# One decoder layer on Trainium2: attention values stationary, probabilities streaming, already divided by their sums

## The reference

```python
xn = rms_norm(h, norm1_w);  proj = xn @ w_in          # q, k, v, gated-linear-attention parts, gate_a, gate_g
p  = softmax(concat([s_meta, s_band, sink]))          # 8 heads, 2 kv heads, window 128, 16 meta keys, 1 sink
o  = p_band @ v_band + p_meta @ v_meta                # per head, 64 wide
y_attn = o @ w_attn_branch;  y_gla = og @ w_gla_branch
merged = sigmoid(gate_a) * y_attn + sigmoid(gate_g) * y_gla
h = h + merged @ w_out
h = h + hierarchical_moe(rms_norm(h, norm2_w))        # 32 experts, 2 per token
```

## Time and profile before

| | us |
|---|---|
| median of the timed runs | 701.44 |
| the profiled execution, its own time | 705.6 |
| its span, first to last instruction | 703.7 |
| attention with the gate chunks and unit (18, u) | about 183 to 330 |
| branch products, merge | about 324 to 372 |
| output product, router | about 372 to 440 |
| experts | about 441 to 703.7 |

### The profile page before, as it was taken

One profiled execution on the slowest core, in us unless ns is written; L12 is line 12 of the kernel. 1 busy time (PEld: TensorE's weight loads), 2 busy tenths in 40 slices (PEclk: granted clock), 3 DMA queues, 4 the chain that ended last, 5 costly groups with the idle time before them and its releaser, 6 DMA issues.

```text
span 703.7 us, 11219 instructions
## 1 busy us (share of the span) xinstructions
PE 670.2 (95%) x4523; PEld 512.8 (73%) x4523; DVE 384.8 (55%) x717; ACT 202.1 (29%) x426; POOL 103.1 (15%) x131
## 2 busy tenths in 40 slices
PE   4999999999999999999999993999999999999998
PEld 2579999888788888888779992656566575756564
DVE  3537224687888777776764556352625253442515
ACT  4337123223533434332333333110111202020102
POOL 3400006788500000000000011110101010110000
PEclk9799999999999999999999996899999999999999
DMA  7432211301122111111347107799999999999953
GB/s 232 138 98 77 66 61 61 107 14 61 61 61 61 60 61 61 61 61 60 104 137 299 61 31 300 305 414 385 414 402 412 403 411 407 403 422 401 418 212 119
DMA packets 49797, 139.32 MB, mean 198 GB/s; under 512 B 6066, under 2 KB 28099, under 8 KB 41556
## 3 DMA queue, kind: packets, MB, share of 16 engines
q1 hardware_dynamic: 47298, 134.36, 50.3%
q0 software_dynamic: 2304, 4.20, 1.6%
q10 hardware_dynamic: 146, 0.07, 0.1%
HBM read 138.61 MB, written 4.19 MB: 203 GB/s over the span
## 4 chain that ended last, share of the span: by engine, by line
PE 86%; DVE 6%; ACT 3%; issue 2%; DMA 2%; POOL 0%; POOLq 0%; ACTq 0%; DVEq 0%
PE bank L881 16%; PE bank L562 13%; PE bank L563 12%; PE bank L564 12%; PE bank L894 8%; PE bank L989 7%; PE bank L789 2%; DVE y_lo L1688 1%; PE bank L762 1%; PE bank L788 1%; PE bank L787 1%; PE bank L722 1%; PE bank L726 1%; ACT whi L1098 1%; DVE sig_a L1436 1%
## 5 line engine op out<-in xcount | busy, mean ns | idle before, releaser
L1374 DVE TENSOR_TENSOR wlo<-wraw,whi 128x2048 fp32r<-128x2048 f32 (+1 forms) x26 | 58.7, 2258 | 30.9 <-ACT whi L1098 30.9
L562 PE MATMUL bank<-whi,xhi 128*128 128x256 f32 (+1 forms) x256 | 73.3, 286 | 0.0
L564 PE MATMUL bank<-whi,xlo 128*128 128x256 f32 (+1 forms) x256 | 71.7, 280 | 0.0
L563 PE MATMUL bank<-wlo,xhi 128*128 128x256 f32 (+1 forms) x256 | 71.7, 280 | 0.0
L562 PE MATMUL bank<-xhi,whi 128*128 128x512 f32 (+2 forms) x176 | 69.5, 399 | 1.6 <-DVE wlo L1374 1.6
L563 PE MATMUL bank<-xlo,whi 128*128 128x512 f32 (+2 forms) x176 | 68.2, 391 | 0.0
L564 PE MATMUL bank<-xhi,wlo 128*128 128x512 f32 (+2 forms) x176 | 67.6, 388 | 0.0
L881 PE MATMUL bank<-wgate,xgT 128*64 128x256 f32 x512 | 60.5, 390 | 1.3 <-DVE xgT L1656 1.0
L881 PE MATMUL bank<-wup,xgT 128*64 128x256 f32 x512 | 58.4, 381 | 0.0
L894 PE MATMUL bank<-wdown,hT 128*64 128x512 f32 x256 | 58.1, 595 | 0.0
L1098 ACT ACTIVATE whi<-wraw 128x2048 fp32r<-128x2048 f32 (+1 forms) x26 | 47.8, 1842 | 25.9 <-PE bank L564 18.7
(11 more groups left out here) (291 smaller groups left out, 1305.4 us busy)
## 6 DMA issues: line engine op xcount, KB each, us to landing
wgate<-in_expert_w_gate SPq DMA_DIRECT2D x32, 1024.0 KB, 7.4
wup<-in_expert_w_up SPq DMA_DIRECT2D x32, 1024.0 KB, 9.6
wdown<-in_expert_w_down SPq DMA_DIRECT2D x32, 1024.0 KB, 17.4
wraw<-in_w_in SPq DMA_DIRECT2D x17, 1024.0 KB, 5.6
wraw<-in_w_out SPq DMA_DIRECT2D x4, 1024.0 KB, 5.4
h<-in_x SPq DMA_DIRECT2D x4, 512.0 KB, 5.3
wraw<-in_w_gla_branch SPq DMA_DIRECT2D x2, 1024.0 KB, 5.2
wraw<-in_w_attn_branch SPq DMA_DIRECT2D x2, 1024.0 KB, 5.1
```

What stands on the lines that cost most here:

```text
L562: nc.tensor.matmul(ps, lhi(k), rhi(k), start=(k == 0), stop=False)
L563: nc.tensor.matmul(ps, lhi(k), rlo(k), start=False, stop=False)
L564: last = nc.tensor.matmul(ps, llo(k), rhi(k), start=False, stop=(k == kt - 1))
L1374: nc.vector.tensor_tensor(w_view(wlo[split_buffer(c)], c), w_view(wraw[c % 2], c), w_view(whi[split_buffer(c)], c).bitcast(F32), ALU.subtr ...
```

## The change

The list of steps changes: PV is made for two attention units at once, at the odd ones, and three units after the first of the two; the sigmoid of a gate unit is made one unit later; a new step ("share", b, i) stands behind it; onorm is gone, and oT has no transposes. In "share" VectorE adds sum and sink term of the two heads and takes the reciprocal, and ScalarE multiplies both heads' probabilities by it in place; the transposes wait for that. PV has the values stationary, 64 columns for each kv head, and the transposed probabilities of two units streaming, 256 wide; kv head 0 writes partitions 0 to 63 of the bank and head 1 the others, the two heads' products taking turns. The result has a row per feature, so ScalarE and VectorE take `ohi` and `olo` straight from that bank. The rows of w_attn_branch are reordered on the host for it. `pt` and `ptm` hold two units' probabilities and become twice as long.

```diff
         b, i = pairs[n]
-        return [("PV", b, i)] + ([("onorm", b)] if i == 3 else [])
+        return [("PV", b, i)] + ([("oT", b)] if i == 2 else [])
 
...
             b, i = pairs[n]
-            s += [("unit", c, u)] + (product(n - 2) if n >= 2 else [])
+            s += [("unit", c, u)] + (product(n - 3) if n >= 3 and n % 2 else [])
             s += [("S", b, i)] + ([("PT",) + pairs[n - 1]] if n >= 1 else [])
             if i == 2:
-                s += [("ogT", b)] + ([("oT", b - 1)] if b >= 1 else [])
-            s += [("sig", c, u)]
-    s += [("prep", 19), ("unit", 18, 0)] + product(14) + [("PT",) + pairs[15], ("unit", 18, 1)] + product(15)
-    s += [("unit", 18, 2), ("oT", NB - 1), ("unit", 18, 3)]
+                s += [("ogT", b)]
+            s += [("sig", 10 + (n - 1) // 2, (n - 1) % 2)] if n >= 1 else []
+            s += [("share", b, i)]
+    s += [("prep", 19), ("sig", 17, 1), ("unit", 18, 0), ("PT",) + pairs[15], ("unit", 18, 1)] + product(14)
+    s += [("unit", 18, 2), ("unit", 18, 3)]
     s += [("prep", 20)] + [("unit", 19, u) for u in range(4)]
...
         oglo = at("oglo", Y + 8 * K1, [P, 4, T], F32R)
-        ptm = [at(f"ptm{i}", 81 * K1 + 512 * i, [NM, P]) for i in range(2)]
         place = [Y + 16 * K1]
...
         v_tok = more("v_tok", [P, NB, P])
-        pt = [at(f"pt{i}", place[0] + K1 * i, [P, 256]) for i in range(2)]
+        pt = [at(f"pt{i}", place[0] + 2 * K1 * i, [P, 2, 2 * P]) for i in range(2)]
         k_tok = more("k_tok", [P, NB, P])
-        o_tok = at("o_tok", place[0], [P, 512])
         km = more("km", [NM, CW])
...
         att_stat = more("att_stat", [P, 2, 5, HQ])
+        ptm = [at("ptm0", 81 * K1, [NM, 2 * P]), more("ptm1", [NM, 2 * P])]
         norm1_b = at("norm1_b", G + 24 * K1, [P, D])
...
                             for b in range(NB):
-                                pe.wait_ge(*banks.emptied(("ogT" if name == "wg" else "oT", b)))
+                                pe.wait_ge(*banks.emptied(("ogT" if name == "wg" else "PV", b)))
                         ih, il = (oghi, oglo) if name == "wg" else (ohi, olo)
...
                         pv = banks.take(pe, "O", ("PV", b))
-                    for j in range(2):
-                        pe.wait_ge(*banks.emptied(("PT", b, i, j)))
-                        hd = j * 4 + i
-                        o = pv[:, hd * DH:(hd + 1) * DH]
-                        vc = slice(j * DH, (j + 1) * DH)
-                        if b > 0:
-                            nc.tensor.matmul(o, pt[j][:, 0:128], v_tok[:, b - 1, vc], start=True, stop=False)
-                        nc.tensor.matmul(o, pt[j][:, 128:256], v_tok[:, b, vc], start=(b == 0), stop=False)
-                        last = nc.tensor.matmul(o, ptm[j][:, :], vm[:, vc],
-                                                start=False, stop=True)
+                    for ii in (i, i + 1):
+                        for j in range(2):
+                            pe.wait_ge(*banks.emptied(("PT", b, ii, j)))
+                    heads = [(pv[j * DH:(j + 1) * DH, i * P:(i + 2) * P], slice(j * DH, (j + 1) * DH)) for j in range(2)]
+                    if b > 0:
+                        for j, (o, vc) in enumerate(heads):
+                            nc.tensor.matmul(o, v_tok[:, b - 1, vc], pt[j][:, 0, :], start=True, stop=False)
+                    for j, (o, vc) in enumerate(heads):
+                        nc.tensor.matmul(o, v_tok[:, b, vc], pt[j][:, 1, :], start=(b == 0), stop=False)
+                    for j, (o, vc) in enumerate(heads):
+                        last = nc.tensor.matmul(o, vm[:, vc], ptm[j][:, :], start=False, stop=True)
                     last.then_inc(s_pv, 1)
-                elif kind in ("oT", "ogT"):
+                elif kind == "ogT":
                     b = step[1]
-                    if kind == "oT":
-                        pe.wait_ge(*banks.emptied(("PV", b)))
-                    else:
-                        pe.wait_ge(s_ogn, b + 1)
-                    src = o_tok[:, :] if kind == "oT" else rgs[:, b, :]
+                    pe.wait_ge(s_ogn, b + 1)
                     ps = banks.take(pe, "unit", step)
                     for j in range(4):
-                        last = nc.tensor.transpose(ps[:, j * P:(j + 1) * P], src[:, j * P:(j + 1) * P], ident)
+                        last = nc.tensor.transpose(ps[:, j * P:(j + 1) * P], rgs[:, b, j * P:(j + 1) * P], ident)
                     last.then_inc(banks.done(step), 1)
...
                         nc.scalar.activation(p, p, ACT.Exp, bias=st_[:, 1, :], scale=SCALE,
-                                             accum_out=st_[:, 2, :]).then_inc(s_prob, 1)
+                                             accum_out=st_[:, 2, :]).then_inc(s_sum, 1)
                         nc.scalar.activation(st_[:, 3, :], sinks[:, hd:hd + 1], ACT.Exp,
                                              bias=st_[:, 1, :]).then_inc(s_es, 1)
+                elif kind == "share":
+                    _, b, i = step
+                    act.wait_ge(s_part, 4 * b + i + 1)
+                    for j in range(2):
+                        n = 2 * (4 * b + i) + j
+                        hd = j * 4 + i
+                        p = prob[n % 4][:, 128 if b == 0 else 0:272]
+                        nc.scalar.activation(p, p, ACT.Copy, scale=att_stat[:, b % 2, 4, hd:hd + 1]).then_inc(s_prob, 1)
                 elif kind == "PT":
...
                     act.wait_ge(*banks.filled(name))
-                    if 4 * b + i:
-                        act.wait_ge(s_pv, 4 * b + i)
+                    if 4 * b + i >= 2:
+                        act.wait_ge(s_pv, (4 * b + i) // 2)
                     ps = banks.get(name)
-                    c0 = 128 if b == 0 else 0
-                    nc.scalar.activation(pt[0][:, c0:256], ps[:, c0:256], ACT.Copy)
-                    nc.scalar.activation(ptm[0][:, :], ps[0:NM, 256:384], ACT.Copy).then_inc(banks.read(name), 1)
+                    k0, tok = 1 if b == 0 else 0, slice(i % 2 * P, (i % 2 + 1) * P)
+                    keys = ps[:, k0 * P:2 * P].rearrange("p (k t) -> p k t", t=P)
+                    nc.scalar.activation(pt[0][:, k0:2, tok], keys, ACT.Copy)
+                    nc.scalar.activation(ptm[0][:, tok], ps[0:NM, 256:384], ACT.Copy).then_inc(banks.read(name), 1)
                 elif kind in ("oT", "ogT"):
                     b = step[1]
-                    act.wait_ge(*banks.filled(step))
+                    name = ("PV", b) if kind == "oT" else step
+                    act.wait_ge(*((s_pv, 2 * (b + 1)) if kind == "oT" else banks.filled(step)))
                     dst, s = (ohi, s_ohi) if kind == "oT" else (oghi, s_oghi)
-                    ps = banks.get(step)[:, :].rearrange("p (j t) -> p j t", j=4)
+                    ps = banks.get(name)[:, :].rearrange("p (j t) -> p j t", j=4)
                     nc.scalar.activation(dst[:, :, b * P:(b + 1) * P], ps, ACT.Copy).then_inc(s, 1)
...
                     dve.wait_ge(*banks.filled(name))
-                    if 4 * b + i:
-                        dve.wait_ge(s_pv, 4 * b + i)
+                    if 4 * b + i >= 2:
+                        dve.wait_ge(s_pv, (4 * b + i) // 2)
                     ps = banks.get(name)
-                    c0 = 128 if b == 0 else 0
-                    nc.vector.tensor_copy(pt[1][:, c0:256], ps[:, c0:256])
-                    nc.vector.tensor_copy(ptm[1][:, :], ps[0:NM, 256:384]).then_inc(banks.read(name), 1)
-                elif kind == "onorm":
-                    b = step[1]
-                    st_ = att_stat[:, b % 2, :, :]
-                    dve.wait_ge(s_es, 8 * (b + 1))
-                    link(nc.vector.tensor_tensor(st_[:, 4, :], st_[:, 2, :], st_[:, 3, :], ALU.add))
-                    link(nc.vector.reciprocal(st_[:, 4, :], st_[:, 4, :]))
-                    dve.wait_ge(s_pv, 4 * (b + 1))
-                    if b:
-                        dve.wait_ge(*banks.filled(("oT", b - 1)))
-                    nc.vector.tensor_tensor(o_tok[:, :].rearrange("p (h d) -> p h d", d=DH),
-                                            banks.get(("PV", b))[:, :].rearrange("p (h d) -> p h d", d=DH),
-                                            st_[:, 4, :].unsqueeze(2).to_broadcast([P, HQ, DH]), ALU.mult)\
-                        .then_inc(banks.read(("PV", b)), 1)
+                    k0, tok = 1 if b == 0 else 0, slice(i % 2 * P, (i % 2 + 1) * P)
+                    keys = ps[:, k0 * P:2 * P].rearrange("p (k t) -> p k t", t=P)
+                    nc.vector.tensor_copy(pt[1][:, k0:2, tok], keys)
+                    nc.vector.tensor_copy(ptm[1][:, tok], ps[0:NM, 256:384]).then_inc(banks.read(name), 1)
+                elif kind == "share":
+                    _, b, i = step
+                    n = 4 * b + i
+                    sums, sink, both = (att_stat[:, b % 2, k, i:HQ:4] for k in (2, 3, 4))
+                    dve.wait_ge(s_es, 2 * (n + 1))
```

(10 more changed lines are left out.)

## The result

The changed kernel takes 722.6 us (median of 4 runs, 720.98 to 722.88), the kernel before, run beside it, 701.1 us (4 runs, 700.72 to 701.48): ratio 1.0276, 95% interval 1.0253 to 1.0298. It is 21.5 us slower. The prediction was slower by 13.8 us, 715.2 us; the measured time lies 2.1 us above its range. A later repeat gave 722.23 us, ratio 1.0286 (1.0265 to 1.0308).

The account below looks back on a forecast made before the run. TensorE was taken to bound the kernel before, VectorE and ScalarE in turn after the change. Delay of 11.7 us plus clock 2.1 made 13.8; added to the 701.44 us median, 715.2 us, range 709.5 to 720.5.

Parts of the forecast that it names:

- TensorE has 16 us less to do: Attention products and transposes: 27.9 us removed, 12 us of two-unit PV added; TensorE alone would win about 16 us.
- VectorE and ScalarE become the bound by order: Gate blocks: share behind the sigmoid delays ScalarE's Copies and conversions, VectorE waits; +5.5 us at the start of chunk 18.
- TensorE stays the bound: Rival for the gate blocks: conversions ready as today, TensorE's 16 us come out, 685.5 us; chance 0.05.
- The round of 37.4 us: VectorE's time per block of four units: 28.66 us of work plus 8.7 of waits, against 36.2 today.
- the upper of the bounds: ScalarE's scaled Copies in share: between 0.36 and 0.52 us each, middle 0.43 taken; bounds give +9.9 and +14.2 us.
- the prediction's own walk: Each engine followed in program order from the stage's start to the last split of the merged rows: +11.7 us.
- The tail: Chunk 18: last PV waits behind split and postponed sigmoid, +6.3 us, TensorE still for about 6.0.
- The clock: After the 6 us stop in chunk 18 the granted clock falls to 0.50: +2.1 us, bounds 0 and 5.
- a rival with a chance of 0.08: Clock also falls in the blocks' 3.3 us stops, three more times 2.1 us: 721.5 us; chance 0.08.
- There TensorE has 5 us a block to spare: Gate blocks: TensorE's slack of 5 us, given as the reason against the half clock costing time after shorter stops.
- The sum: Whole kernel: 11.7 us from the walk plus 2.1 for the clock, 13.8 us slower.

Follow-up runs that it names:

- The last kernel: Changed kernel with share ahead of each unit's own sigmoid, and chunk 18's last probability copies and unit (18, 2) moved earlier: 688.28 us, ratio 0.9805.
- early conversion: Changed kernel with ScalarE converting the next chunk's weights one step earlier, before its Copies; share left behind the sigmoid: 698.01 us.
- share first: Changed kernel with share ahead of the sigmoid and each sigmoid back in its own unit: 693.02 us.
- stops filled: Changed kernel with unread transposes where TensorE stood still, 28 in each block's third unit and 50 before the last PV: 719.37 us.
- tail reordered: Changed kernel with chunk 18's last sigmoid and probability copies ahead of chunk 19's split, and unit (18, 2) ahead of the last PV: 713.34 us.

## Why the prediction was right, and where its sizes were off

**TensorE has 16 us less to do.** Right. The last kernel takes 12.9 us less in the gates and 2.5 in the tail than before, 15.4 together. PV of two units takes 1.59 us (1.6 predicted). The twelve records alone are 1.31 at the 0.109 us of the earlier trace rows, which leaves 0.28 us for entering and leaving the shape. The Trainium skill (TensorEngine Tiling (Array Packing), section When to Use Tiling) recommends this swap, and its section Key Properties warns of the drain; the runs agree with the advice only where VectorE and ScalarE have their steps in the right order: 21.5 us slower in the one, 12.8 us faster in the other.

**VectorE and ScalarE become the bound by order.** Right, and shown twice: by moving share, and by moving the conversion. The rival "TensorE stays the bound" named its point of decision, 5.6 us of waits a block; the early conversion removed 2 x 2.80 and got 32.83 us, share first 32.17, with TensorE busy throughout (31.8 predicted for its round).

**The round of 37.4 us.** This is the step that was too small, and the main reason why the measured time lies above the range: 38.65 measured. Waits 2.80 + 2.81 for `whi` (2 x 2.69), 1.97 for `ohi` (1.86), 1.33 for `oghi` (1.4), and 0.93 for late transposes, where the prediction had 0.1: together 9.84 against 8.7; the work is the other 28.8 (28.66). So 0.83 of the 1.25 us is that last wait. Of it 0.51 is the half clock (0.42 remain with the stops filled). Of the other 0.74 us, 0.66 lie in waits behind the Copies: 0.32 at the transposes, 0.23 at the two splits, 0.11 at the output. They are put down to the Copies themselves, which took 0.51 us busy and 0.42 to the next start by their rows (two in 0.93 or 0.94, `whi` 0.84 us after the first starts, where 0.66 was walked). That is the upper of the bounds (0.52 and about 0.42), where the middle was taken, and by the prediction's own walk the upper bound is worth 2.5 us of the sum (14.2 in place of 11.7). That share was not tested by itself. The last 0.08 is work and rounding. By the third block the delay was 4.4 us where 3.0 was predicted, two blocks added 2.45 each where 1.25 was: 9.35 at (18, 0) against 5.5.

**The tail.** The order of events was right, step by step. TensorE was idle for 5.90 us before the last PV (6.0 predicted), and (18, 2) came at 18.10 us (16.2): the copies ended 0.5 us later than walked, and the last PV, at half clock, took 2.95 us in place of 1.6. From (18, 0) on the prediction has 11.7 - 5.5 = 6.2 us and the clock's 2.1, together 8.3; 9.0 was measured.

**The clock.** It did fall to 0.50 after the stop in chunk 18. The price of 2.1 us was about right: filling the stops shortened the tail by 1.9, with the two reservations made there. It fell as well after each of the blocks' stops of 3.0 to 3.1 us, which the prediction held to be a rival with a chance of 0.08 and a price of 2.1 us each. That rival's 721.5 us comes nearest to the measured time, but by luck: filling the four stops of the gates gave back 0.9 us and not 6.3. TensorE makes up most of what it loses there: with the tail reordered the half clock lasted longer (mean 0.94 in the gates against 0.96), and the gates took 146.16 us, against 146.20. It doesn't make up all of it, since the transposes stand right behind the stop and VectorE waits for them. "There TensorE has 5 us a block to spare" was the wrong reason: it has them on the average, not at that place.

**The sum.** 20.1 us between the two profiled executions (722.64 and 702.51) against 13.8 predicted: 3.9 more in the gates, 0.7 in the tail, 1.1 at one wait in the router, 0.6 in the experts. The last two the prediction put at nothing, and their cause is open. The other 1.4 us of the 21.5 is that the second profile of before lies that much above the median of the first comparison.

**Open.** The wait in the router is for the rows gathered by DMA, before and after the change, in TensorE's timeline:

```profile
435.66 1.97 PE L875 MATMUL bank<-cst,xg 128*128 128x128 f32 x8 [3.75 <-DMA xg<-rows_hbm,row_no]
```

```profile
455.21 1.97 PE L874 MATMUL bank<-cst,xg 128*128 128x128 f32 x8 [4.86 <-DMA xg<-rows_hbm,row_no]
```

The instructions there are the same, and so is their distance before the wait. Of the nine kernels with the new attention three have the short one (3.64 to 3.82 us), six and the repeat the long one (4.60 to 4.86). What decides it was not found. In the best kernel it takes back 0.9 us.

## What to carry to other kernels

Before work is handed over from an engine that is full to engines that have time, look where in their program the new instructions stand and what is queued behind them: here two Copies of 0.4 us waited for VectorE and held back a conversion of 1.9 us that VectorE needed for its next step, and moving one step of the list made +21 us into -3. A step that another engine waits for goes ahead of a long piece that nobody waits for. A mean slack of an engine is no cover for its slowest moment, and of the bounds of an unknown cost take the upper one when it lies in a loop that closes on itself.

## What the runs showed of the hardware that was not expected

- ScalarE's Copy with a scale per partition costs as much as an Exp of that shape: two of 128x272 in 0.93 us (0.51 busy and 0.42 to the next start), against 0.52 busy for the Exp. A Copy of 128x256 without one is 0.36; it also reads a bank and not a tile, and which of the two makes the difference was not tested.
- Stops of TensorE of 3.1 us between stretches of dense products were followed by a granted clock of 0.50 and 0.51 (the windows of two of the blocks above), and with transposes in their place the clock was 1.00 through the block. Shorter stops went either way: 2.78 us (share first, own sigmoid) and 2.49 (stops filled, chunk 18) were followed by 0.50 and 0.51, 2.44 (conversion early, at 305.65) was not.
- Of the half clock what stands right behind the stop was paid for most visibly: the six transposes, 0.21 us apart in place of 0.105, and the last PV, 2.95 us (336.22 to 339.17) in place of 1.59.
